# Expert-spread operands with the expert index innermost, and three layers multiplied in plain fp32

## What is computed

```python
h = first_block(x, ...)                      # HGRN2 layer, then forgetting attention, each with an output product
xn = rms_norm_2(h, norm1_g)
proj = xn @ w_in + b_in                      # 26 tiles of 128 columns: 16 convolution, k, v, 8 q
conv_out = conv_group(proj[..., :2048], ...) # gate, causal convolution with 31 taps, layer norm, silu
attn_out = swa_group(q, k, v, ...)           # banded attention, window 128
h = h + concat([conv_out, attn_out]) @ w_out # 16 tiles
h = h + peer(rms_norm_2(h, norm2_g), ...)    # 8 heads choose 16 of 16384 experts each, by products of sub-keys
```

## Time and profile before

| | |
|---|---|
| median of 3 runs | 3547.64 us (3545.72 to 3549.3) |
| profiled execution | 3545.76 us; span on the core 3543.9 us |
| TensorE busy | 3275.0 us (92%), 25842 matmuls |
| VectorE, ScalarE, POOL busy | 2021.0 us, 1694.6 us, 763.9 us |
| mean granted TensorE clock | 0.931 of full |
| chain that ended last | TensorE 83%, VectorE 9%, issue 4%, ScalarE 3% |

### The profile page before, as it was taken

The page is one execution under the profiler, slowest core; times in us unless marked ns, Lnnn a source line. Parts: engine busy times, 40 slices in busy tenths (PEclk is TensorE's granted clock), DMA queues, the critical chain, the costliest instruction groups (busy, mean ns, idle before and its releaser), DMA issues.

```text
span 3543.9 us, 66107 instructions
## 1 busy us (share of the span) xinstructions
PE 3275.0 (92%) x25842; PEld 3210.5 (91%) x25842; DVE 2021.0 (57%) x3416; ACT 1694.6 (48%) x2641; POOL 763.9 (22%) x329
## 2 busy tenths in 40 slices
PE   7999989999999855769769999999999999999999
PEld 7999989999998855659669999999999999999999
DVE  4555546544445799566996555554445555554444
ACT  5666655666775433664212344444442244444443
POOL 3333324444343665314530000000000000000000
PEclk9999989999999987869877799999998799999999
DMA  5343334444333422214321155555553145555553
GB/s 190 140 142 137 135 107 160 165 168 152 140 132 122 174 89 83 72 50 176 119 89 61 70 187 189 180 179 186 178 185 112 60 155 189 179 181 185 179 185 134
DMA packets 72271, 506.35 MB, mean 143 GB/s; under 512 B 7904, under 2 KB 10592, under 8 KB 11232
## 3 DMA queue, kind: packets, MB, share of 16 engines
q1 hardware_dynamic: 71584, 503.09, 40.2%
q10 hardware_dynamic: 576, 1.72, 0.1%
HBM read 502.69 MB, written 2.10 MB: 142 GB/s over the span
## 4 chain that ended last, share of the span: by engine, by line
PE 83%; DVE 9%; issue 4%; ACT 3%; DMA 0%; DVEq 0%; SPq 0%; ACTq 0%
PE bank L422 11%; PE bank L424 10%; PE bank L423 10%; PE bank L1741 7%; PE bank L1743 7%; PE bank L1742 7%; PE bank L1917 7%; PE bank L1916 7%; PE bank L1915 7%; PE bank L1730 5%; DVE c_acc L1163 2%; PE bank L625 1%; DVE r_oh L1591 0%; ACT c_pr L1377 0%; PE bank L640 0%
## 5 line engine op out<-in xcount | busy, mean ns | idle before, releaser
L399 ACT ACTIVATE whi<-raw 128x1024 fp32r<-128x1024 f32 x950 | 998.0, 1057 | 1259.5 <-PE bank L424 518.4
L406 DVE TENSOR_TENSOR wlo<-raw,whi 128x1024 fp32r<-128x1024 f32 x682 | 823.7, 1223 | 393.9 <-ACT whi L399 393.7
L406 POOL TENSOR_TENSOR wlo<-raw,whi 128x1024 fp32r<-128x1024 f32 x268 | 710.9, 2657 | 1071.0 <-ACT whi L399 1065.4
L422 PE MATMUL bank<-xa_hi,whi 128*128 128x272 f32 (+1 forms) x2064 | 608.1, 295 | 3.5 <-DVE xa_lo L1398 3.0
L424 PE MATMUL bank<-xa_hi,wlo 128*128 128x272 f32 (+1 forms) x2064 | 599.5, 290 | 0.0
L423 PE MATMUL bank<-xa_lo,whi 128*128 128x272 f32 (+1 forms) x2064 | 597.8, 290 | 0.0
L1741 PE MATMUL bank<-xb_hi,whi 128*128 128x256 f32 x2048 | 590.0, 288 | 1.1 <-DVE hT L1962 1.1
L1742 PE MATMUL bank<-xb_lo,whi 128*128 128x256 f32 x2048 | 589.6, 288 | 0.0
L1743 PE MATMUL bank<-xb_hi,wlo 128*128 128x256 f32 x2048 | 588.5, 287 | 0.0
L1916 PE MATMUL bank<-e_coef_lo,whi 128*128 128x256 f32 x2048 | 579.6, 283 | 0.0
L1915 PE MATMUL bank<-e_coef_hi,whi 128*128 128x256 f32 x2048 | 579.6, 283 | 0.0
(11 more groups left out here) (381 smaller groups left out, 4748.5 us busy)
## 6 DMA issues: line engine op xcount, KB each, us to landing
raw<-in_w SPq DMA_DIRECT2D x219, 1024.0 KB, 4.8
raw<-in_u SPq DMA_DIRECT2D x128, 1024.0 KB, 4.8
raw<-in_v SPq DMA_DIRECT2D x128, 1024.0 KB, 5.3
hT<-in_hT SPq DMA_DIRECT2D x4, 544.0 KB, 8.3
out<-hT SPq DMA_DIRECT2D x8, 256.0 KB, 2.7
r_keys<-in_keys ACTq DMA_DIRECT2D x1, 1024.0 KB, 4.8
c_mask<-in_masks ACTq DMA_DIRECT2D x1, 320.0 KB, 2.9
params<-in_params SPq DMA_DIRECT2D x1, 238.5 KB, 2.6
```

What stands on the lines that cost most here:

```text
L399: act.activation(whi[:, (2 * t.q + half) % 4, :], raw[:, t.q, half * 1024:(half + 1) * 1024], ACT.Copy).then_inc(w_hi_done, 1)
L406: eng.tensor_tensor(wlo[:, slot, :], raw[:, t.q, half * 1024:(half + 1) * 1024], whi[:, slot, :].bitcast(F32), ALU.subtract).then_inc(w_lo ...
L422: te.matmul(ps, hi, x[0][:, kk, cols], start=(kk == 0), stop=False)
```

## The change

The tiles from `T_CONV` to `T_PEERQ` (convolution, attention, output product; 42 tiles) are multiplied by a new `project_fp32` directly from `raw` and from fp32 activations `xn1` and `xn2`, laid over `xb` hi and `xa` hi. Nothing splits these weights or activations: the copies at L399, the subtractions at L406, the lo parts at L507 (for `T_BOUT`'s output), L1347, L1388 and L1398 go for them. The next stage's first tile is split during the last tile of the output product, both halves on POOL. SP loads a tile in this stretch when the tile four before it has been multiplied instead of split. In the spread phase `e.row`, `e.one`, `e.col` hold the sub-key innermost; the slots and gates are stored twice in a row, and VectorE's operands are read as pairs, so that the innermost run of each operand has two elements. The replicated table of sub-key numbers becomes a single row of 128. The waits on `w_lo_done` and `w_hi_done` are counted without the 42 tiles.

```diff
-        SPREAD_BYTES = STEP * (SUBKEYS + SUBKEYS // 2 + 4 * SEG)
+        SPREAD_BYTES = STEP * (SUBKEYS + 4 * SEG)
-            e.iota_rep = tensor(st, "e_iota_rep", [P, SUBKEYS, STEP], BF16)
-            e.row = tensor(st, "e_row", [P, 2, SUBKEYS, STEP], BF16)
-            e.one = tensor(st, "e_one", [P, 2, SEG, STEP], BF16)
-            e.col = tensor(st, "e_col", [P, 2, 3, SEG, STEP], BF16)
+            e.row = tensor(st, "e_row", [P, 2, STEP, SUBKEYS], BF16)
+            e.one = tensor(st, "e_one", [P, 2, STEP, SEG], BF16)
+            e.col = tensor(st, "e_col", [P, 2, 3, STEP, SEG], BF16)
...
+        def project_fp32(te, t, x, n):
+
+            te.wait_ge(evacuated, t.n - 1)
+            te.wait_ge(w_loaded[t.q], 16 * t.m + 16)
+            ps = bank[t.q % 2][:, 0:n]
+            for kk in range(KT):
+                last = te.matmul(ps, raw[:, t.q, kk * P:(kk + 1) * P], x[:, kk, 0:n], start=(kk == 0),
+                                 stop=(kk == KT - 1))
+                if kk % 8 == 7:
+                    last.then_inc(halves_done, 1)
...
-        OUT = ((T_AOUT, xb, cols_all, "kv_norm", xa, 1), (T_BOUT, xa, cols_q, "norm1", xb, 3),
-               (T_WOUT, xa, cols_q, "norm2", xb, 4))
+        OUT = ((T_AOUT, xb, cols_all, "kv_norm", xa, 1), (T_BOUT, xa, cols_q, "norm1", xn1, 3),
+               (T_WOUT, xn2, cols_q, "norm2", xb, 4))
...
+            if base == T_WOUT:
+                te.wait_ge(S.cm, CONV_T)
+                te.wait_ge(S.m, NQ)
...
-                    if within(j - 1, KT):
+                    if within(j - 1, KT) and base != T_BOUT:
                         ve.wait_ge(x_hi_done, SPLITS[base] + j)
                         ve.scalar_tensor_tensor(at3(y[1], j - 1, slice(0, n)), at3(hT, j - 1, cols),
...
         def conv_tensor(te, ch):
             def body(i):
                 for s in range(4):
-                    project(te, Tile(T_CONV, i, s), xb, slice(0, SEQ))
+                    t = Tile(T_CONV, i, s)
+                    if static(t.n) and t.n == T_CONV:
+                        te.wait_ge(xn1_done, KT)
+                    project_fp32(te, t, xn1, SEQ)
...
         def conv_pool(po, ch):
-            po.wait_ge(w_lo_done[0], T_CONV + 1)
             def body(i):
                 for s in range(4):
-                    for half in range(2):
-                        split_lo(po, Tile(T_CONV, i, s).next(), half)
                     if s % 2 and within(2 * i + s // 2 - 1, CONV_T):
                         side_sum(po, 2 * i + s // 2)
...
         def swa_scalar(act, ch):
             for s in range(NSLOT + 6):
-                if s < NSLOT:
-                    split_hi(act, Tile(T_SWK, 0, s).next())
...
-                if s - 2 in CONV_SLOTS:
-                    lo_part(CONV_SLOTS.index(s - 2), c.cm[:])
...
-                    ve.wait_ge(x_split, SPLITS[T_CONV] + xcount[0])
-                    ve.tensor_copy(c.mm[:], B_RO[:, SEQ:2 * SEQ]).then_inc(S.m, 1)
+                    ve.tensor_copy(xn2[:, CONV_T + j, :], B_RO[:, SEQ:2 * SEQ]).then_inc(S.m, 1)
...
-            act.activation(e.slots[:], bank[3][:].rearrange("p (a b) -> p a b", a=2), ACT.Copy)
+            for w in range(2):
+                act.activation(e.slots[:, w, :, :],
+                               bank[3][:, w * SEQ:(w + 1) * SEQ].rearrange("p (a b) -> p a b", b=1)
+                               .broadcast_to([P, SEQ, 2]), ACT.Copy)
...
-                    last = te.matmul(ps, e.row[:, b, :, k], e.col[:, b, w, :, k], start=(w == 0), stop=(w == 2))
+                    last = te.matmul(ps, e.row[:, b, k, :], e.col[:, b, w, k, :], start=(w == 0), stop=(w == 2))
...
-            ve.tensor_tensor(e.one[:, b, :, :], e.iota_rep[:, g_ * SEG:(g_ + 1) * SEG, :],
-                             per_column(e.slots[:, 1, now], SEG), ALU.is_equal).then_inc(one_set, 1)
+            ve.tensor_tensor(pairs(e.one[:, b, :, :]), keys(g_ * SEG, SEG), per_token(e.slots[:, 1, now, :], SEG),
+                             ALU.is_equal).then_inc(one_set, 1)
...
+        def pairs(ap):
+            return ap.rearrange("p t (n b) -> p t n b", b=2)
+
+        def keys(at, n):
+            return e.iota[:, at:at + n].rearrange("p (t n b) -> p t n b", t=1, b=2).broadcast_to([P, STEP, n // 2, 2])
+
+        def per_token(ap, n):
+            return ap.rearrange("p t (n b) -> p t n b", n=1).broadcast_to([P, STEP, n // 2, 2])
...
-            weights(4, TILES, lambda n: w_in[bass.ds(n, 1)].rearrange("a p c -> p a c"))
+            weights(4, T_CONV + 4, w_tile, split)
+            weights(T_CONV + 4, T_PEERQ + 4, w_tile, used)
+            weights(T_PEERQ + 4, TILES, w_tile, split_late)
```

More of the change, by code:

```diff
@@ L54 @@
 TILES = T_PEERQ + 2 * PEER_HEADS
+NATIVE = T_PEERQ - T_CONV
 SUBKEYS = 128
@@ L215, in build @@
         root = tensor(ctx, "root", [P, L])
+        e = Named()
+        with ExitStack() as st:
+            e.hid = tensor(st, "e_hid", [P, 2, SEQ])
+        with ExitStack() as st:
+            e.coef_hi = tensor(st, "e_coef_hi", [P, 2, SEQ], F32R)
+        with ExitStack() as st:
+            e.rest = tensor(st, "e_rest", [P, 2, SEQ])
         sq2 = tensor(ctx, "sq2", [P, 2, L])
@@ L222, in build @@
         hT = tensor(ctx, "hT", [P, KT, L])
+        with ExitStack() as st:
+            xn1 = tensor(st, "xn1", [P, KT, SEQ])
         xb = (tensor(ctx, "xb_hi", [P, KT, L], F32R), tensor(ctx, "xb_lo", [P, KT, L], F32R))
         innermost = ExitStack()
+        with ExitStack() as st:
+            xn2 = tensor(st, "xn2", [P, KT, SEQ])
         xa = (tensor(innermost, "xa_hi", [P, KT, L], F32R), tensor(innermost, "xa_lo", [P, KT, L], F32R))
@@ L397, in split_hi @@
             for half in range(2):
-                need(act, halves_done, 2 * t.n + half - 3)
+                need(act, halves_done, 2 * t.n + half - 3 if not static(t.n) or t.n not in RESUMED else 2 * T_CONV)
                 act.activation(whi[:, (2 * t.q + half) % 4, :], raw[:, t.q, half * 1024:(half + 1) * 1024],
@@ L461, in out_tensor, with splits_next @@
             te.matmul(SUM[:, 0:n], con("ones"), root[:, 0:n], start=True, stop=True).then_inc(sum_done, 1)
+        xn1_done = sem("xn1_done")
+        def splits_next(base, j):
+            if base == T_AOUT:
+                return within(j, KT)
+            if base == T_BOUT:
+                return within(j, KT - 1)
+            return static(j) and j == KT - 1
         def out_scalar(act, ch, spec):
@@ L530, in body @@
                 for s in range(4):
-                    for half in halves:
-                        split_lo(po, Tile(base, i, s).next(), half)
-            ch.run(body, 0, 4, 0)
+                    if splits_next(base, 4 * i + s):
+                        for half in halves:
+                            split_lo(po, Tile(base, i, s).next(), half)
+            if base == T_WOUT:
+                po.wait_ge(w_lo_done[0], T_CONV)
+                body(KT // 4 - 1)
+            else:
+                ch.run(body, 0, 3, 1)
         zeros_l = zt[:]
@@ L1532, in swa_pool @@
             for s in range(NSLOT):
-                for half in range(2):
-                    split_lo(po, Tile(T_SWK, 0, s).next(), half)
                 if s == 0:
@@ L1813, in operands @@
+            ve.tensor_tensor(pairs(e.row[:, b, :, :]), keys(0, SUBKEYS), per_token(e.slots[:, 0, now, :], SUBKEYS),
+                             ALU.is_equal)
             ve.wait_ge(one_set, at + 1)
             for w in range(3):
-                last = ve.tensor_tensor(e.col[:, b, w, :, :], e.one[:, b, :, :], per_column(e.gates[:, w, now], SEG),
-                                        ALU.mult)
+                last = ve.tensor_tensor(pairs(e.col[:, b, w, :, :]), pairs(e.one[:, b, :, :]),
+                                        per_token(e.gates[:, w, now, :], SEG), ALU.mult)
@@ L1830, in gate_parts, with twice @@
-            ch.link(ve.tensor_copy(e.gates[:, 2, :], e.rest[:, 1, :]))
+            def twice(ap):
+                return ap.rearrange("p (a b) -> p a b", b=1).broadcast_to([P, SEQ, 2])
+            ve.tensor_copy(e.iota[:], con("iota"))
+            ch.link(ve.tensor_copy(e.gates[:, 0, :, :], twice(e.slot_gate)))
+            ch.link(ve.tensor_tensor(e.rest[:, 0, :], e.slot_gate, e.gates[:, 0, :, 0], ALU.subtract))
+            ch.link(ve.tensor_copy(e.gates[:, 1, :, :], twice(e.rest[:, 0, :])))
@@ L1832, in both_lo @@
+            ch.link(ve.tensor_tensor(e.rest[:, 1, :], e.rest[:, 0, :], e.gates[:, 1, :, 0], ALU.subtract))
+            ch.link(ve.tensor_copy(e.gates[:, 2, :, :], twice(e.rest[:, 1, :])))
         def both_lo(ve, t):
@@ L1977, in _, with split, used, split_late @@
                 sp.dma_start(raw[:, q, :], w_in[q]).then_inc(w_loaded[q], 16)
-            def weights(n0, n1, source):
+            def split(n):
+                for half in range(2):
+                    sp.wait_ge(w_lo_done[half], n - 3)
+            def used(n):
+                sp.wait_ge(halves_done, 2 * n - 6)
+            def split_late(n):
```

(6 more changed lines are left out.)

105 lines of the change are left out of this document (41 added, 64 removed).

## The result

The changed kernel takes 3362.44 us (median of 4 runs, 3360.41 to 3364.13), the kernel before 3547.1 beside it: a ratio of 0.948, 95% interval 0.9467 to 0.9491. The profiled execution took 3362.66 us, its span is 3360.8.

A forecast was written before the change was run, and what follows sets the result against it. Output product and spread were taken as bound by TensorE, convolution by VectorE slowed by POOL, attention by handovers. Terms -61 - 8.5 - 7 + 19.5 - 71 = -128 us gave 3420 us; own range 3370 to 3458, 3468 with two rivals.

The forecast's parts named there:

- The spread: Spread bursts: contiguous operands at 0.060 us a matmul instead of 0.121, burst 7.1 us; -71 us, bounds -98 and 0.
- I take 0.060, the lower bound at half clock, since bursts run mostly there: Spread matmul time chosen between 0.030 and 0.121 us; 1.44 us a step, not 2.91.
- My lower bound of 0.030: Spread matmul at 64/256 of a split pass, at full clock; 5.5 us a burst, -98 us.
- with its stretch at half clock: Up tile behind a spread burst, taken at 7.6 us.
- my -55: Spread term by the skill's 81 ns a pair: step 1.94 us, burst 8.1, instead of -71.
- VectorE is late next: Spread bursts: TensorE would wait twice a burst for operands VectorE makes in 2.04 us a step.
- Convolution: Convolution: without POOL's splits a turn takes 16.2 us instead of 24.33, TensorE keeping up; net -61 us.
- What is late next is TensorE: Attention slots: TensorE's own list of 11.6 us sets the pace; slots 12.5 us instead of 14.2.
- The bound of 11: Attention slots: 11 us each if small matmuls shrink with a better clock; -16 us.
- The three terms: Attention: head 0, five slots -8.5 us, the six slots behind -7 us.
- Output product: Output product: bound by TensorE before and after, 112.4 us in place of 92.9; +19.5 us.
- Rivals: Spread matmul unchanged 3491 (0.08); VectorE's paired rate lost 3465 (0.10); TensorE bound 3463 (0.08); slower, low clock 3641 (0.03).

The follow-up runs named there:

- e5: Changed kernel with spread matmuls reading, by step number, both operands contiguously, moving operand, weights or both at stride 8; 3428.39 us.
- e1: Kernel before with only the spread's new operand layout and the new places in memory; 3431.1 us beside 3550.39.
- e3: Kernel before with only the tensor e.coef_hi moved, to byte 22240 over sq2; 3532.64 us.
- e9: Changed kernel with POOL again doing four half-tile subtractions each convolution turn, on data nothing uses; 3419.49 us.
- e12: Changed kernel with every second channel block left out of the attention's projections; 3357.25 us.
- e14: Changed kernel with the output product in split form again and the attention's results cut again into two parts; 3348.84 us.
- e8: Changed kernel with coef_hi 32 bytes further on, at byte 22272; 3370.18 us.
- e7: Kernel before with coef_hi, coef_lo and e.coef 32 bytes further on; 3530.52 us.
- e15: Changed kernel with 32 empty bytes ahead of xb, shifting all moving operands of split matmuls but coef_hi; 3359.92 us.
- e16: Changed kernel with spread steps paired around a half tile, output product in split form and 32 bytes ahead of coef_lo; 3309.28 us, median of 4.

## Why the prediction was wrong, by its own steps

Between the -128 forecast and the -183 of the account lie 55 us: 32.5 in the spread, 14.7 in the expert tiles, 12.4 ahead of the output product, less 4.6 lost in that product and the routing. The first two are the steps that failed.

**The spread.** Mechanism right: the stride of 16 bytes on the moving operand held the matmul at 0.121 us (e5). The step that failed is the term I chose between the bounds: "I take 0.060, the lower bound at half clock, since bursts run mostly there". Contiguous matmuls take 29 ns at full clock and 53 at half, and 27 of 32 steps ran at full: the low clock belonged to the strided bursts and went with them (0.71 to 0.90, in e1 as well). I had carried the clock of the old bursts over to the new ones. My lower bound of 0.030 was the value: most bursts are 5.66 us (my own sum with 0.030 is 5.64, not the 5.5 that I wrote), some 6.2, and the first, with `both_lo` between its operands, 9.25. Sixteen of them gave 89 us, where 0.060 said 71. The rest is a second step, a term at nothing: the tile behind a burst was kept at 7.6 us "with its stretch at half clock"; it takes 6.5 on the average, 14 us for fourteen tiles. Together -103.5. (The Trainium skill, TensorE: Matmul & The Clock Gate, "Back-to-back issue gap", gives the gap of an isolated matmul as N/2.4 + 2.5 ns warm and N/1.2 cold, an estimate of 29.2 and 53.3 for 64 columns; the trace has 29 at full clock and 53 at half, in streams of weight loads and matmuls. Its 81 ns for such pairs is for 128 moving columns, which no run here has; carried over to 64, as for my -55, it did not hold.) "VectorE is late next" held: twice a burst TensorE waits for `e.col`.

**Expert tiles.** Costed at nothing, since no line of theirs changes. What failed is the reading of the diff: it moves a tensor, and I read its allocation only for room. It gave 14.7 us (13.4 of them by one tensor's place, e3), without which the time would be 3377, inside the range.

**Convolution.** The turn came out at 15.4, not 16.2, from the right cause. POOL's splits cost VectorE 0.83 of their length (e9); the side sum costs 3.25 us, not 3.9, though its own rows grew to 5.86: 0.55 each, so one factor does not serve all of POOL's work. With the eighth turn that is 9 us more than forecast. (The sum itself had a slip: 197.4 - 133 is 64.4, not 63.) TensorE did keep up, at clock 0.99.

**Attention.** "What is late next is TensorE" was wrong (e12): the slot closes through ScalarE and VectorE in 11.1 us. The bound of 11 was on record for another reason, a better clock. The three terms missed in both directions, counted between the same read-outs of q: up to the third 32.4 us became 35.0 (I had no change; TensorE's projections are on the path there, by e12), the five slots behind it 72.5 became 54.6 (-17.9 for -8.5), the rest up to the output product 50.1 became 46.0 (-4.1 for -7). That is -19.4 for -15.5.

**Output product.** +20.0 for +19.5. **Routing.** +4.1 for 0. TensorE's wait ahead of it:

```profile
PE bank L433 <- DMA r_keys<-in_keys: 7.1, 1, 7.1
```

It was 4.9 before. SP, held back by tiles that are now freed by being multiplied, issues its loads at the moment that `r_keys` is fetched; the wait is 2.2 us longer, of which 1.6 are left at the next read-out. The other 2.5 come at later tiles, in TensorE's waits for VectorE behind the searches (60.6 us for 58.1); why is open. I had counted SP's queue for the tiles and not for its neighbour. That the loads are the cause of the first part is read from their times; e14, with the output product and its loads as before, loses the 4.1 whole and has the 4.9 and 58.1 back.

**Rivals.** None came about. The time lies below the range, where only the bounds of terms stood for "better than thought": the spread came out at its low bound and a little beyond, and the expert tiles, a term without bounds, were added to it.

## What to carry to other kernels

Lay out what a bf16 matmul streams so that neighbours in its columns are neighbours in memory; with 128 weights and 64 moving columns a stride on the moving operand doubled the matmul's time at 4 elements, and cost about twice what it did on the weights. Where a small matmul becomes four times faster, ask at once who feeds it and what its clock will be, and give the feeder work of TensorE to hide behind (a half tile between pairs of steps was worth 35 us). A diff's allocations are part of the change: look up which operands of hot loops move.

## What the runs showed of the hardware that was not expected

- 32 bytes decide 1 to 3 ns of a 118 ns fp32r matmul: 120.0 ns (118.9 in e8) with both moving operands at multiples of 64 bytes, 116.7 with both at odd multiples of 32 (e7, e15, e16), in the down halves; in the up halves the shift cost 0.6 (e15).
- Strided weights are cheaper than a strided moving operand: 60 against 115 ns at 8 elements, though they are 128 columns against 64. The moving side pays 1.8 ns for each 16 bytes that it touches (59 ns at stride 4, 115 at 8).
- POOL's adds over 128x1024, 512 and 256 cost VectorE 0.55 of their length, its subtractions of 128x1024 cost 0.83.
- In the slot shown ScalarE's piece of 1.28 us at 1425.77 is the load of a function table (Ln to Exp): 1.28 of the chain's 11.1 us, and a second load lies beside it. From the timeline of that slot:

```profile
1425.77 1.28 ACT L1400 ACT_TABLE_LOAD   x1
1433.53 1.28 ACT L1424 ACT_TABLE_LOAD   x1
```
